# The TensorE program of an expert-choice MoE, written out instead of looped

## The chip, the cores and the metric

The kernel runs on one core of a Trainium2 chip. Its metric is the device time of one execution, in microseconds (us), given as the median of three runs. The profile is of one further execution.

## The reference

One inference step of a backbone with one layer. 512 latent tokens (`x_sample`) and 128 context tokens (`x_prompt`), each 1024 wide, go through a mixing sub-layer (pooling and retention) and then a mixture of 16 experts in which each expert picks its tokens: the top 64 latent and the top 16 context tokens. All weights are float32.

```python
aff = softmax(h @ w_router)                      # one row of 16 scores per token
gate, idx = top_k(swapaxes(aff, 1, 2), cap)      # each expert picks its tokens
xs = h[idx]
hid = silu(xs @ w_gate) * (xs @ w_up)            # 1024 -> 2816, per expert
out = (hid @ w_down) * gate                      # 2816 -> 1024, per expert
y = zeros.at[idx].add(out)
```

The outputs are the normed rows of both token sets and the retention states of the context.

## The kernel before

The mixing sub-layer comes first (up to about 600 us) and is not touched. After it come the experts. An expert's hidden width of 2816 is cut in two, so that there are 32 half experts (`STEPS = 2 * NE`). The weights of a half expert come in 12 pieces of 1.0 to 1.6 MB: four of the gate matrix (`g`), four of the up matrix (`u`), four of the down matrix (`d`). They are read through a ring of 12 buffers (`RING`, the tile `ring`). SyncE issues each load at L568 (gate and up) or L575 (down), once TensorE has counted the buffer's last reading on the semaphore `e_used`; a load that has landed is counted on `e_landed[slot]`.

TensorE runs the pieces in the order of `STEP`: g0, d0, g1, d1, g2, d2, d3, g3, u0, u1, u2, u3. The gate and up pieces are those of half expert r + 1, the down pieces those of half expert r. The gate product is done in two parts: units of tokens against the weights themselves (L2396) and units against sums of weight blocks (L2403). The sums are made by VectorE (L1715, tile `sums`) from the gate pieces in the ring, ahead of TensorE. The down products are at L2386 and the up products at L2414. Every half expert issues 776 pairs of a weight load and a matmul by the counts of the trace.

TensorE's first eight pieces stand ahead of the loop. Then the loop `pe.Fori(0, STEPS - 1)` at L2423, a loop that the engine itself executes, goes 31 times through the 12 pieces, and its waits are on semaphore values that are computed from the loop's register r. The last down pieces are behind the loop (L2458). SyncE, GpSimd, VectorE and ScalarE have loops of their own over 15 experts (L594, L823, L1885, L1217), with two half experts in each pass.

In each pass GpSimd gathers the token rows of the next expert (L756 and L766, indirect DMAs into `x_g`) and adds the rows of the expert before to a scratch in DRAM (L800 and L803). The gather lies in the even half experts, r = 0, 2, 4 and so on up to 28.

Behind the experts GpSimd reads the summed rows into `y_tile` (L837). That waits for the landing of the last down piece, since `y_tile` lies where ring buffers were. ScalarE and VectorE norm the rows, and the outputs are written.

Of the kernel before, what the change touches and what calls it, by code (L numbers as in the profile page):

```python
# [54 lines left out]
STEPS = 2 * NE  # L55
# [191 lines left out]
def build(nc, x_prompt, x_sample, c, state_ret, c_ctx, w_ada, b_ada, norm1_g, w_in, w_pool, pool_scale,  # L247
# [3 lines left out]
    with ctx:  # L251
# [1686 lines left out]
        def _(pe):  # L1938
# [365 lines left out]
            def gate_up(up, i, slot, tiles):  # L2304

                w = ring[slot][:, 0:2 * FH].rearrange("p (k f) -> p k f", f=FH)
                for kk in range(2):
                    k = 2 * i + kk
                    for x in tiles:
                        for c in range(4):  # L2310
                            ins = mm(bank[UP_BANK[x] if up else x][c * Q:(c + 1) * Q, 0:FC], xs_t[:, x, k * Q:(k + 1) * Q],  # L2311
                                     w[:, kk, c * FC:(c + 1) * FC], start=k == 0, stop=k == KT - 1)
                return ins
# [65 lines left out]
            def down(i, slot):  # L2379

                w = ring[slot][:, 0:DOWN_N[i] * D].rearrange("p (f d) -> p f d", d=D)
                for j in range(DOWN_N[i]):
                    f = DOWN_AT[i] + j
                    for x in range(NX):
                        for c in range(4):
                            ins = mm(bank[5 + x // 2][c * Q:(c + 1) * Q, x % 2 * DC:(x % 2 + 1) * DC],  # L2386
                                     hid_t[:, f, x * Q:(x + 1) * Q], w[:, j, c * DC:(c + 1) * DC],
                                     start=f == 0 and x != 1, stop=f == FTH - 1, skip_group_check=True)
                ins.then_inc(e_used, 1)

            def gate(r, i, slot):

                w = ring[slot][:, 0:2 * FH].rearrange("p (k c n f) -> p k c n f", k=2, c=4, n=2)
                for u, b, o, k, n in OWN_AT:
                    for c in range(4):
                        mm(bank[b][c * Q:(c + 1) * Q, o:o + FN], unit(u)[:, i, :], w[:, k, c, n, :],  # L2396
                           start=i == 0 and o == 0, stop=i == KT // 2 - 1, skip_group_check=True)
                for j in range(N_SUM):
                    b, o = SUM_AT[j]
                    if j % 2 == 0:  # L2400
                        pe.wait_ge(sums_done, 4 * N_SUM * r + N_SUM * i + j + 2)
                    for c in range(4):
                        ins = mm(bank[b][c * Q:(c + 1) * Q, o:o + FN], unit(j)[:, i, :], sums[:, (N_SUM * i + j) % SUM_SLOTS, c, :],  # L2403
                                 start=i == 0 and j % 2 == 0, stop=i == KT // 2 - 1, skip_group_check=True)
                ins.then_inc(e_used, 1)

            def up(i, slot):

                w = ring[slot][:, 0:2 * FH].rearrange("p (k f) -> p k f", f=FH)
                for x in range(NX) if i else reversed(range(NX)):  # L2410
                    for kk in range(2):
                        k = 2 * i + kk
                        for c in range(4):
                            ins = mm(bank[UP_BANK[x]][c * Q:(c + 1) * Q, 0:FC], xs_t[:, x, k * Q:(k + 1) * Q],  # L2414
                                     w[:, kk, c * FC:(c + 1) * FC], start=k == 0, stop=k == KT - 1)
                    if i == 3 and x < 2:
                        ins.then_inc(e_up, 1)
                ins.then_inc(e_used, 1)

            pe.wait_ge(e_xt, 1)  # L2420
            for t in range(FIRST):
                gate_up(t // 4, t % 4, t, (0, 1)).then_inc(e_used, 1)
            with pe.Fori(0, STEPS - 1) as r:  # L2423
                for t in range(RING):
                    slot = (FIRST + t) % RING
                    kind, i = STEP[t]
                    if t == 0:
                        pe.wait_ge(x_dve, r + 1)
                        pe.wait_ge(x_act, r + 1)
                        pe.wait_ge(e_silu, 2 * r + 2)  # L2430
                        pe.wait_ge(e_comb, r + 1)
                    if (kind, i) == ("d", 0):
                        pe.wait_ge(e_hid, NX * r + NX)
                    if (kind, i) == ("u", 0):
                        pe.wait_ge(e_xt, r + 2)
                        pe.wait_ge(e_out, NX * r + NX)
                    pe.wait_ge(e_landed[slot], 16 * r + (16 if slot >= FIRST else 32))
                    if kind == "g":
                        gate(r, i, slot)
                    elif kind == "d":  # L2440
                        down(i, slot)
                    else:
                        up(i, slot)
# [86 lines left out]
```

## Time and profile before

| what | value |
|---|---|
| median of 3 runs | 1986.44 us (1984.62 to 1986.86) |
| profiled execution, its own time | 1986.42 us |
| its span, first to last instruction | 1984.6 us |
| TensorE busy in matmuls | 1910.4 us, 96% of the span |
| VectorE, ScalarE, GpSimd busy | 1207.5, 395.4, 394.6 us |
| mean granted TensorE clock | 0.989 of full speed |
| read from HBM, written to it | 632.47 MB, 14.40 MB |

The span leaves out 1.8 us that the execution's own time has around it. A share of busy time is a mean over stages: the experts take about 640 to 1953 us, and there both TensorE and the DMA engines are busy nearly all the time. The page says of every DMA queue how many packets it moved, how many MB, and what share of the 16 DMA engines' time they took. One of the queues carries instructions. Times of rows count from the span's start.

### The profile page before, as it was taken

To read this page: it belongs to the slowest core of one execution; us is meant where nothing else is said; L and a number is where in the kernel's file an instruction comes from. 1 tells how busy PE (TensorE), PEld (TensorE's weight loads), DVE (VectorE), ACT (ScalarE), POOL (GpSimd) and SP (SyncE) were. 2 spreads that over 40 slices of the span, in tenths; PEclk is the share of its full clock that TensorE was granted. 3 is DMA by queue.
4 is the path that set the end of the run, shared out by engine and by line. 5 is a ranking of instruction groups with operands and counts; after the bars stand their busy time and mean duration, and the time that the engine had idled before them with its cause. 6 is when DMAs were issued, how large, how long until landed. Compare 5 with 4: busy or idle time off the path is not lost.

```text
span 1984.6 us, 64364 instructions
## 1 busy us (share of the span) xinstructions
PE 1910.4 (96%) x28594; PEld 1604.4 (81%) x28594; DVE 1207.5 (61%) x1969; ACT 395.4 (20%) x909; POOL 394.6 (20%) x406
## 2 busy tenths in 40 slices
PE   8999999999997999999999999999999999999996
PEld 5888899999873888788877778779777687877874
DVE  3532441232556777687676867767677676867764
ACT  4331333122320111111111211112111111211113
POOL 3032019000411130311303113030211303112012
PEclk9999999999998999999999999999999999999998
DMA  8244542312359999999999999999999999999997
GB/s 334 86 161 151 176 129 64 107 51 79 127 220 363 412 407 419 408 411 415 408 418 409 414 412 411 415 407 420 407 411 416 407 419 408 412 414 412 414 411 288
DMA packets 150463, 647.58 MB, mean 326 GB/s; under 512 B 11420, under 2 KB 56344, under 8 KB 134024
## 3 DMA queue, kind: packets, MB, share of 16 engines
q1 hardware_dynamic: 134576, 617.71, 77.5%
q0 software_dynamic: 15648, 29.02, 5.0%
q8 instruction: 42, 0.69, 0.1%
q14 instruction: 13, 0.11, 0.0%
q10 hardware_dynamic: 184, 0.06, 0.0%
HBM read 632.47 MB, written 14.40 MB: 326 GB/s over the span
## 4 chain that ended last, share of the span: by engine, by line
PE 76%; DMA 12%; DVE 4%; SPq 3%; issue 3%; ACT 1%; POOL 0%; POOLq 0%; DVEq 0%; ACTq 0%
PE bank L2386 17%; PE bank L2414 16%; PE bank L1985 16%; PE bank L2403 9%; DMA ring<-in_w_exp_gate_dram 9%; PE bank L2396 6%; PE bank L2106 3%; PE bank L2252 2%; SPq L568 2%; DMA ring<-in_w_exp_down_dram 1%; PE bank L2311 1%; SPq L575 1%; PE bank L1956 1%; PE bank L1967 1%; DMA x_in<-in_x_sample_dram 1%
## 5 line engine op out<-in xcount | busy, mean ns | idle before, releaser
L1715 DVE TENSOR_TENSOR sums<-ring 128x704 f32<-128x704 f32 x744 | 608.5, 886 | 191.8 <-PE bank L2403 168.2
L2386 PE MATMUL bank<-ring,hid_t 128*32 128x256 f32 x8184 | 480.4, 379 | 12.9 <-DVE hid_t L1787 7.2
L2414 PE MATMUL bank<-ring,xs_t 128*32 128x352 f32 x5952 | 453.1, 459 | 0.0
L2386 PEld LDWEIGHTS bank<-ring,hid_t 128*32 128x32 f32 x8184 | 380.6, 110 | 79.4 <-issue 9.8
L2414 PEld LDWEIGHTS bank<-ring,xs_t 128*32 128x32 f32 x5952 | 307.5, 110 | 128.3 <-issue 7.6
L2403 PE MATMUL bank<-sums,xu_a 128*32 128x176 f32 x5952 | 296.5, 313 | 18.3 <-issue 17.8
L2403 PEld LDWEIGHTS bank<-sums,xu_a 128*32 128x32 f32 x5952 | 241.9, 110 | 42.6 <-issue 40.3
L791 POOL TENSOR_TENSOR small<-kpow 128x2 f32<-128x2 f32 x31 | 10.4, 334 | 993.1 <-DVE out_rows L1846 868.1
L1167 ACT ACTIVATE v_both<-bank 128x176 f32<-128x176 f32 x31 | 9.9, 318 | 856.0 <-PE bank L2403 856.0
L2396 PE MATMUL bank<-ring,xu_a 128*32 128x176 f32 x1984 | 173.8, 313 | 0.0
L1985 PE MATMUL bank<-act_hi,wt_hi 128*128 128x320 f32 x448 | 138.8, 310 | 0.8 <-DVE rtmp L1526 0.8
L1276 DVE TENSOR_TENSOR wt_lo<-raw_t,wt_hi 128x2048 fp32r<-128x2048 f32 x25 | 57.6, 2303 | 134.6 <-ACT wt_hi L888 134.6
L1985 PE MATMUL bank<-act_lo,wt_hi 128*128 128x320 f32 x448 | 138.4, 309 | 0.0
L1985 PE MATMUL bank<-act_hi,wt_lo 128*128 128x320 f32 x448 | 138.4, 309 | 0.0
L2396 PE MATMUL bank<-ring,xu_b 128*32 128x176 f32 x1984 | 123.9, 313 | 0.0
L2396 PEld LDWEIGHTS bank<-ring,xu_a 128*32 128x32 f32 x1984 | 114.1, 110 | 9.8 <-issue 0.3
L2396 PEld LDWEIGHTS bank<-ring,xu_b 128*32 128x32 f32 x1984 | 94.2, 110 | 1.6
L803 POOL DMA_INDIRECT acc_scratch<-out_rows,idx_scatter x60 | 83.2, 1386 | 18.3 <-issue 18.3
L1985 PEld LDWEIGHTS bank<-act_hi,wt_hi 128*128 128x128 f32 x448 | 84.1, 188 | 1.3 <-issue 1.3
L1985 PEld LDWEIGHTS bank<-act_lo,wt_hi 128*128 128x128 f32 x448 | 84.1, 188 | 0.0
L1985 PEld LDWEIGHTS bank<-act_hi,wt_lo 128*128 128x128 f32 x448 | 84.1, 188 | 0.0
L1189 ACT ACTIVATE silu_g<-bank 128x352 f32<-128x352 f32 x31 | 14.4, 465 | 233.2 <-PE bank L2414 233.2
(366 smaller groups left out, 2398.5 us busy)
## 6 DMA issues: line engine op xcount, KB each, us to landing
ring<-in_w_exp_gate_dram SPq DMA_DIRECT2D x128, 1408.0 KB
ring<-in_w_exp_up_dram SPq DMA_DIRECT2D x128, 1408.0 KB
ring<-in_w_exp_down_dram SPq DMA_DIRECT2D x96, 1536.0 KB
ring<-in_w_exp_down_dram SPq DMA_DIRECT2D x32, 1024.0 KB
raw_t<-in_w_ada_dram SPq DMA_DIRECT2D x16, 1024.0 KB, 5.3
raw_t<-in_w_in_dram SPq DMA_DIRECT2D x14, 1024.0 KB, 5.2
a_raw<-in_w_ada_dram SPq DMA_DIRECT2D x8, 1024.0 KB, 16.5
raw_t<-in_w_branch_gate_dram SPq DMA_DIRECT2D x8, 1024.0 KB, 5.4
```

The source lines that it names most:

```text
L568: sp.dma_start(ring[slot][:, 0:2 * FH].rearrange("p (k f) -> p k f", f=FH), src).then_inc(e_landed[slot], 16)
L575: sp.dma_start(ring[slot][:, 0:DOWN_N[i] * D], src).then_inc(e_landed[slot], 16)
L803: pool.indirect_dma_start(acc_rows, bass.IndirectOffsetOnAxis(idx_scatter[0:C_P, 2 + c:3 + c], 0), out_rows[prompt_slots(c), 2, :], None, ...
L1276: nc.vector.tensor_tensor(lo_of(b), raw(INDEX[b]), hi_of(b).bitcast(F32), ALU.subtract).then_inc(w_lo_done, 1)
L1715: nc.vector.tensor_tensor(sums[:, (N_SUM * i + j) % SUM_SLOTS], w[:, k, :, n, :], w[:, kk, :, nn, :], ALU.add if sign > 0 else ALU.subtrac ...
L1985: ins = mm(out, a, b, start=i == 0, stop=i == count - 1)
L2106: return mm(o[:, :], a, w, start=i == first and kk == 0 and z == 0, stop=i == last and kk == 1 and z == 2)
L2252: return mm(bank[WO_BANKS[i % 3][c]][:, :], a, w, start=k == 0 and z == 0, stop=k == KT - 1 and z == 2)
L2386: ins = mm(bank[5 + x // 2][c * Q:(c + 1) * Q, x % 2 * DC:(x % 2 + 1) * DC], hid_t[:, f, x * Q:(x + 1) * Q], w[:, j, c * DC:(c + 1) * DC], ...
L2396: mm(bank[b][c * Q:(c + 1) * Q, o:o + FN], unit(u)[:, i, :], w[:, k, c, n, :], start=i == 0 and o == 0, stop=i == KT // 2 - 1, skip_group_ ...
L2403: ins = mm(bank[b][c * Q:(c + 1) * Q, o:o + FN], unit(j)[:, i, :], sums[:, (N_SUM * i + j) % SUM_SLOTS, c, :], start=i == 0 and j % 2 == 0 ...
L2414: ins = mm(bank[UP_BANK[x]][c * Q:(c + 1) * Q, 0:FC], xs_t[:, x, k * Q:(k + 1) * Q], w[:, kk, c * FC:(c + 1) * FC], start=k == 0, stop=k = ...
```

## The change

The loop on the engine becomes a loop in the Python program that builds the kernel, so that TensorE's instructions for the 31 half experts stand one after another, and the values waited for are constants.

```diff
@@ -2420,7 +2420,7 @@
             pe.wait_ge(e_xt, 1)
             for t in range(FIRST):
                 gate_up(t // 4, t % 4, t, (0, 1)).then_inc(e_used, 1)
-            with pe.Fori(0, STEPS - 1) as r:
+            for r in range(STEPS - 1):
                 for t in range(RING):
                     slot = (FIRST + t) % RING
                     kind, i = STEP[t]
```

The order of the matmuls and the conditions of the waits stay the same. The loops of the other engines stay.

## Rows read from the trace of the kernel before

**Rows 1.** The page's 40 slices of the span: busy tenths, and GB/s.
```profile
PE   8999999999997999999999999999999999999996
...
DMA  8244542312359999999999999999999999999997
GB/s 334 86 161 151 176 129 64 107 51 79 127 220 363 412 407 419 408 411 415 408 418 409 414 412 411 415 407 420 407 411 416 407 419 408 412 414 412 414 411 288
```
**Rows 2.** The windows view: us, busy us by engine (x instructions), PEclk, DMA share, GB/s.
```profile
640.00:684.40 44.40, 42.34 (x788) 35.20 (x780) 30.59 (x52) 5.93 (x20) 7.14 (x7) 1.00 1.02 411
684.40:768.60 84.20, 82.50 (x1558) 71.00 (x1553) 61.59 (x97) 12.43 (x37) 15.78 (x14) 1.00 1.02 412
...
1189.10:1273.40 84.30, 82.47 (x1560) 66.34 (x1556) 61.32 (x97) 12.44 (x37) 15.85 (x14) 1.00 1.02 412
...
1699.40:1785.10 85.70, 82.83 (x1557) 68.02 (x1553) 61.32 (x97) 12.43 (x37) 16.29 (x14) 1.00 1.02 412
...
1870.40:1910.80 40.40, 40.40 (x784) 36.97 (x780) 29.30 (x44) 6.04 (x16) 8.97 (x7) 1.00 1.03 410
```
**Rows 3.** The chain that ended last, in order of time: start us, us, what.
```profile
1283.66 3.67 PE bank L2386 x68
...
1370.63 26.23 DMA ring<-in_w_exp_gate_dram
...
1883.67 26.31 DMA ring<-in_w_exp_gate_dram
...
1927.19 29.27 DMA ring<-in_w_exp_down_dram
1956.75 4.43 DMA y_tile<-acc_scratch
```
**Rows 4.** The groups view of TensorE's lines in the loop: xcount, busy us, mean ns.
```profile
L2386 PE MATMUL bank<-ring,hid_t 128*32 128x256 f32 x8184 | 480.4, 379 | 12.9 <-DVE hid_t L1787 7.2 <-issue 5.0 <-DVE hid_t L1822 0.6
L2414 PE MATMUL bank<-ring,xs_t 128*32 128x352 f32 x5952 | 453.1, 459 | 0.0
...
L2403 PE MATMUL bank<-sums,xu_a 128*32 128x176 f32 x5952 | 296.5, 313 | 18.3 <-issue 17.8
...
L2396 PE MATMUL bank<-ring,xu_a 128*32 128x176 f32 x1984 | 173.8, 313 | 0.0
```
**Rows 5.** The page's queues: packets, MB, share; and its first section.
```profile
PE 1910.4 (96%) x28594; PEld 1604.4 (81%) x28594; DVE 1207.5 (61%) x1969; ACT 395.4 (20%) x909; POOL 394.6 (20%) x406
...
q8 instruction: 42, 0.69, 0.1%
```
**Rows 6.** The DMA view of 700 to 1950 us: the queues.
```profile
q1 hardware_dynamic: 80115, 505.67, 98.4%
q0 software_dynamic: 9437, 9.76, 3.6%
q14 instruction: 2, 0.02, 0.0%
```
**Rows 7.** The DMA view of 640 to 684.4 us, half expert 0.
```profile
q1 hardware_dynamic: 2849, 17.83, 98.5%
q0 software_dynamic: 224, 0.33, 2.1%
q8 instruction: 7, 0.11, 1.0%
```
**Rows 8.** The DMA view, queue q1, from 724.8 and from 893 us, 44.4 us each.
```profile
q1 hardware_dynamic: 2893, 18.08, 99.2%
...
q1 hardware_dynamic: 2854, 18.12, 99.4%
```
**Rows 9.** The DMA view in narrow windows: 628.4 to 629.3, 701.3 to 702.2, 702.2 to 703.5 us.
```profile
DMA packets 64, 0.32 MB, mean 360 GB/s; under 512 B 16, under 2 KB 16, under 8 KB 56
...
DMA packets 65, 0.39 MB, mean 437 GB/s; under 512 B 7, under 2 KB 7, under 8 KB 55
...
DMA packets 75, 0.59 MB, mean 455 GB/s; under 512 B 9, under 2 KB 9, under 8 KB 42
```
**Rows 10.** The timeline of TensorE's matmuls across the end of a pass at 1061.33 us.
```profile
1047.13 14.43 PE L2414 MATMUL bank<-ring,xs_t 128*32 128x352 f32 x192
1061.33 0.52 PE L2396 MATMUL bank<-ring,xu_a 128*32 128x176 f32 x8
```
**Rows 11.** The source view of L2403: what TensorE's idle time before it ended with.
```profile
  issue: 58.1, 136
```

## The prediction

> **What bounds the kernel now.** I read the slices first. From the fourteenth slice on, about 645 us, both TensorE and the DMA engines stand at nine tenths or more to the end [rows 1]. Two engines can't both be the bound over the same stretch unless they are nearly equal, so the question is which of them gives way to the other.
>
> The windows by pairs of half experts answer that. I cut the stretch at TensorE's own steps, where its first gate matmul begins (640.4, 684.4, 768.6 us and so on). The reader should see two lengths. Until about 1357 us a pair takes 84.0 to 84.3 us, and after it 85.3 to 85.7 [rows 2]. The DMA share and the rate are the same in both: 1.02 of the 16 engines' time and 412 GB/s. So the DMA engines work at their limit all the way, from before 700 us, while TensorE's pace changes. A half expert with no gather takes 40.4 us at best, with TensorE busy through all of it [rows 2] (the last row).
>
> The weights thus come more slowly than TensorE uses them in the first eight pairs. It lives on a store of landed pieces, since the ring had been filled ahead. Once the store is down to what VectorE needs for its sums, the DMA engines set the pace. The chain of waits says the same. In the experts it first holds only matmuls, still at 1283 us. From 1370 us it goes, once in each pair, through 26.2 us of a transfer into the ring, seven times, and it ends with the last down piece and the load of `y_tile` behind it [rows 3]. The span's end is therefore the end of the weight stream plus a fixed 28 us: 1927.2 + 29.3 = 1956.5, and 1984.6 less that.
>
> What follows for any edit: time taken from TensorE in this stage buys nothing, and every microsecond given to the DMA engines for something else comes back in full, also in the first part, where TensorE is the slower to notice.
>
> **What is removed.** Gone are 31 jumps back and the register operations that computed the waits' values. Their price on the path: nothing. Across the end of a pass the last up matmul starts just ahead of 1061.33, and the row of up matmuls (1047.13 + 14.43 = 1061.56 us, with the tail of the last) runs into the first gate matmul of the next pass at 1061.33 with no gap [rows 10]. The half expert of 40.4 us busy in 40.4 us has both a jump and all its register waits inside [rows 2]. What covers them is TensorE's queue of matmuls already issued. If that cover were gone, the DMA limit would still stand ahead of it. The bound from the other side is all of TensorE's idle time that ended with nothing but its own issuing, 58.1 us [rows 11]. Its stretches lie in even half experts only, inside the gather, not at the jump, and I give the change none of them: nothing is removed at that place, and the DMA engines would not let the gain through.
>
> **What is added.** The instructions themselves have to be read. First their number. The four lines of the loop have 8184 + 5952 + 5952 matmuls and, at L2396, 1984 for each of two operands [rows 4], so 24056, or 776 pairs in each of 31 passes. The page has 28594 pairs and 42 packets of instructions on queue q8 [rows 5]. If each was read once, written straight it is 28594 - 30 x 776 = 5314 pairs, 10628 instructions, and 10628 / 42 = 253 for a packet of 0.69 / 42 MB = 16.4 KB. That the loop's body is read once and then kept is to be seen directly: 7 packets in the first pass [rows 7], about 1552 / 253 = 6.1 by the count, and not one on q8 in the 1250 us from 700 to 1950 [rows 6]. After the change all 31 passes are like the first: 30 x 1552 / 253 = 184 more packets, 3.0 MB.
>
> The Trainium skill ("Runtime: NRT & Kernel Launch", "Instruction fetch mechanics") has 16 KiB blocks of 256 instructions too, and 128 KiB for TensorE, enough for this body. It also says that crossing a block boundary is mostly hidden, and that a kernel should rather be unrolled, since a jump out of the window stalls. By that rule the change costs nothing or gains, which is among the rivals below.
>
> Then the price of a packet. TensorE doesn't wait for one: it reads ahead, and the first pass shows no gap of its own (42.3 us busy of 44.4, with the gather's idle time in it like every even pass). The price is paid by the weight stream. Two measures bound it.
>
> - Below: the 7 packets took 1.0% of 16 engines' 44.4 us [rows 7], so 0.01 x 16 x 44.4 / 7 = 1.01 us of one engine each. Spread over 16 engines that is 63 ns of the stream.
> - Above: what the stream moved less. In 44.4 us of the first pass q1 moved 17.83 MB [rows 7]. In equal windows placed alike in two later even passes it moved 18.08 and 18.12 [rows 8]. That is 0.25 to 0.29 MB less, at about 408 KB a us 0.61 to 0.71 us, or 88 to 102 ns for each packet.
>
> Is it right to divide by 16? A ring transfer ends with one small packet from each engine. At 628.4 us all 16 of them lie in one 0.9 us window. At 701 us, after the packets of the first pass, 7 engines are on time and 9 come in the 1.3 us behind it [rows 9], some 1.1 us late by the windows' middles. So packets go to one engine after another, each making one more late, and don't pile up on one. A lateness of 1.1 us over 16 engines is 69 ns a packet, between the two measures.
>
> I take 86 ns: close to the measures of the stream itself, since lost ring bytes are what counts, and a little below them because the windows' edges cut pieces. 184 x 0.086 = 15.8 us. The ends are 184 x 0.063 = 11.6 and 184 x 0.102 = 18.8.
>
> The sum: 1986.42 (profiled, 0.02 from the median of the runs) + 15.8 = 2002.2 us. The pair of half experts goes from 85.5 to 85.5 + 12.27 x 0.086 = 86.6 us in the part that the DMA engines set. As the first part's 84.2 falls further behind, the store is used up sooner: it fell 1.3 us a pair over eight pairs, it will fall 2.4, so the chain should turn to ring transfers after four or five pairs, at 1000 to 1100 us instead of 1360.
>
> **The rivals.**
>
> - *The packets are hidden.* If the stream made up for them, say because the engines had slack between pieces, the time would stay at 1986.4. For it speaks only that 3.0 MB is 0.5% of the traffic. Against it: a DMA share of 1.02 with no slack [rows 2] and the late engines [rows 9]. For less than 0.2% (4.0 us) a packet would have to cost under 22 ns. Chance 0.05. That the change doesn't do what it says has no way to happen here that I can see; it would also give this time.
> - *TensorE waits for its instructions.* Reading ahead works in the first pass, but every pass now needs it under a full DMA load. If each of 184 packets stalled it by the 1.01 us that the packet takes, TensorE's pair would be 84.2 + 12.4 = 96.6, and the end 15.5 x (96.6 - 85.5) = 172 us later, about 2158. If it stalls for a tenth of that (1.2 us a pair) it stays under the DMA pace of 86.6 and costs nothing; it decides from 0.2 us a packet on. Chance 0.06, mostly near the lower end.
> - *All packets after the first pass go to one engine.* Then that engine has 184 x 1.01 = 186 us more to do, and as each transfer waits for its slowest share the end is at about 2160. [rows 9] speak against it. Chance 0.01.
> - *Faster, through TensorE.* The jump and the register operations keep TensorE's sequencer from running ahead, and this is why it starves during gathers. Written out it would not, and up to 58.1 us of idle time [rows 11] would go: 1928. The mechanism decides only if the DMA engines could move in 80.8 us (twice 40.4) what they now move in 85.5 us at 412 GB/s, which is 436 GB/s, and no window shows it [rows 2]. Chance 0.02.
> - *Faster, through the jump.* Each jump back waits for a packet of its target, 1.01 us: 30 us less, 1956. The skill's rule on jumps, named above, would have this. No packet on q8 for 1250 us [rows 6] and no gap at 1061.33 [rows 10] rule it out as it stands. Chance 0.01.
>
> **How the numbers follow.** My forecast has 0.85: slower by 11.6 to 18.8 us, 1998.0 to 2005.2. About 4 us (0.2%) is what a measurement of this kernel tells from no change. Slower: 0.85 + 0.06 + 0.01 = 0.92. Same: 0.05. Faster: 0.03. For the range I widen the bounds of the price by 2 us below, for packets that cost less where the stream is refilled between passes, and by 3.8 above for short stalls of TensorE: 1996.0 to 2009.0.
>
> **What the profile after should show.** About 226 packets (3.7 MB) on q8, and some 6 of them in each 42 us from 640 to 1950. A DMA share of 1.02 as before, and a rate of about 409 GB/s where it was 412. Half experts with no gather still at 40.4 us before the DMA engines take over, and pairs of 86.6 us after. The last down piece landing near 1972 us, and 28 us behind it. TensorE's instructions the same in number. I am wrong if gaps of TensorE stand where packets land, if the pairs stay at 85.5, or if one engine's share grows late without end.

## The result and the profile after

The kernel takes 2018.2 us (median of 4 runs, 2016.6 to 2020.4) where the one before takes 1985.9 (4 runs). The ratio is 1.0164 with a 95% interval of 1.0146 to 1.0182, so 32.4 us slower. The direction was as forecast and the amount was twice the forecast one: 15.8 us had been expected.

The page after, its slices from the head (the granted clock, the DMA engines, the rate):

```profile
PEclk8999999999988999999999999999999999999998
DMA  8254532212369999999999999999999999999995
GB/s 337 80 162 141 175 125 79 89 64 84 138 255 362 414 404 409 413 406 415 405 413 411 409 407 398 412 400 405 408 408 403 396 417 397 404 410 408 405 400 233
...
q8 instruction: 224, 3.67, 0.7%
```

The instruction queue has 182 packets more than in [rows 5], 3.0 MB, where 184 were counted beforehand. The rate starts at about 409 GB/s and is often 396 to 405 in the later slices, where [rows 1] have 407 to 420.

The windows by pairs of half experts, cut again at TensorE's own steps:

```profile
641.60:723.40 81.80, 81.15 (x1557) 50.46 (x1553) 62.28 (x99) 11.96 (x36) 16.64 (x14) 1.00 1.02 409
723.40:804.20 80.80, 80.80 (x1556) 59.36 (x1552) 59.05 (x93) 12.42 (x37) 15.87 (x14) 1.00 1.02 409
804.20:886.60 82.40, 81.15 (x1559) 59.47 (x1555) 59.04 (x95) 12.41 (x37) 16.93 (x14) 1.00 1.02 409
886.60:975.20 88.60, 82.60 (x1556) 67.43 (x1552) 61.98 (x98) 12.43 (x37) 15.89 (x14) 0.96 1.02 411
...
1151.60:1240.30 88.70, 83.65 (x1560) 47.48 (x1556) 61.18 (x96) 12.41 (x37) 16.19 (x14) 0.96 1.01 404
...
1851.90:1940.40 88.50, 83.30 (x1558) 49.63 (x1554) 61.11 (x96) 12.42 (x37) 16.45 (x14) 0.96 1.01 405
```

Two things differ from [rows 2]. The first pairs are at 80.8 to 82.4 us where they were 84.2: TensorE's idle time in the gathers is nearly gone. And from 886.6 to 1851.9 us eleven pairs take 87.75 us each where the forecast was 86.6. In most of those the DMA share has fallen by a hundredth, and the mean granted clock of TensorE is 0.96 to 0.98.

The chain of waits, in order of time:

```profile
775.95 27.44 DMA ring<-in_w_exp_gate_dram
...
1915.31 26.29 DMA ring<-in_w_exp_gate_dram
1959.72 29.63 DMA ring<-in_w_exp_down_dram
1989.64 4.19 DMA y_tile<-acc_scratch
```

It turns to ring transfers at 776 us instead of 1370 [rows 3]. The last down piece lands at 1989.3 and the span ends 27.9 us later, as before. The end is the end of the weight stream here too, so all of the 32.4 us has to be found in the stream.

It is found in two places. From 700 to 1950 us the DMA view of after has this:

```profile
q1 hardware_dynamic: 78785, 496.09, 97.2%
q0 software_dynamic: 9376, 9.51, 3.6%
q8 instruction: 175, 2.87, 0.9%
```

Against 505.67 MB in [rows 6], q1 moved 1.9% less in the same time. Over the 1312 us of the stage in the kernel before (640 to 1952 us) that is 24.9 us. The packets took 0.009 x 16 x 1250 / 175 = 1.03 us each, the 1.01 of before.

The second place is the end of the stream. Windows of 4 us up to the last landing, with each engine's busy time and, at the row's end, the granted clock, the mean DMA share and the rate; before:

```profile
1940.00:1944.00 4.00, 4.00 (x60) 1.81 (x56) 3.37 (x7) 3.41 (x8) 0.03 (x1) 1.00 1.00 422
1944.00:1948.00 4.00, 4.00 (x60) 1.70 (x54) 0.00 (x0) 0.04 (x1) 3.67 (x6) 1.00 1.01 425
1948.00:1952.00 4.00, 4.00 (x60) 1.82 (x56) 0.70 (x2) 0.00 (x0) 1.94 (x2) 1.00 1.02 425
1952.00:1956.00 4.00, 3.72 (x68) 2.20 (x60) 2.99 (x5) 1.95 (x3) 0.00 (x0) 1.00 0.92 322
```

and after:

```profile
1973.00:1977.00 4.00, 4.00 (x60) 1.65 (x56) 3.60 (x7) 3.42 (x9) 0.00 (x0) 1.00 0.50 207
1977.00:1981.00 4.00, 4.00 (x60) 1.60 (x56) 0.00 (x0) 0.27 (x1) 3.50 (x6) 1.00 0.76 294
1981.00:1985.00 4.00, 4.00 (x60) 1.64 (x56) 0.52 (x1) 0.00 (x0) 2.12 (x3) 1.00 0.68 246
1985.00:1989.00 4.00, 3.72 (x64) 2.15 (x60) 3.15 (x5) 1.95 (x3) 0.00 (x0) 1.00 0.40 154
```

Before, the 16 engines work in full until 4 us from the end and finish together. After, about half of them are done some 16 us early, and the last transfers wait for the rest. In the last 16 us the share is short by 0.50, 0.25, 0.34 and 0.52 of 4 us each, 6.4 us per engine. 24.9 + 6.4 = 31.3 of the 32.4 us. So the instruction packets do not lie on all engines alike.

The trace shows directly how they lie. For most transfers into the ring it keeps sixteen times of landing, one for each engine's share (for some a few are missing). The table has how far each share lands behind the transfer's first one, in us; the kernels of the last five rows are described below.

| kernel | first share lands at | seven shares | one share | the other eight |
|---|---|---|---|---|
| before | 702.0 | up to 0.3 | 1.0 | 1.5 to 1.9 |
| before | 1872.5 | up to 0.3 | 1.0 | 1.1 to 1.7 |
| after | 703.0 | up to 0.4 | 1.0 | five 1.5 to 2.0, three 3.0 to 3.3 |
| after | 1112.3 | up to 0.7 | 1.7 | 12.7 to 14.4 |
| after | 1972.6 (the last) | up to 0.3 | 0.3 | 13.7 to 16.8 |
| first8 | 1016.0 | up to 0.7 | 1.9 | 10.5 to 11.3 |
| first8 | 1884.2 | up to 0.6 | 1.7 | 10.3 to 11.4 |
| last15 | 1298.3 | up to 0.3 | 1.6 | 1.6 to 1.9 |
| last15 | 1953.3 (the last) | up to 0.5 | 1.7 | 13.9 to 17.2 |
| light_straight | 1387.8 | up to 0.4 | 0.5 | 0.6 to 2.7 |

From 630 to 689 us eight packets come in the kernel before, and with each of them one more share falls behind, until eight are. In the changed kernel the ninth packet (689.1 us) takes one of the late ones to 3.2 us, and the seven stay where they are. So the packets go round on eight of the sixteen engines. The sixteenth share, 1.0 us late, is so before the second packet comes; what makes it late is not shown.

### The profile page after: what moved, and what is told of

Its sections match the earlier page's. It is cut to its first block, busy times and chain, and to the rows that moved or that the text cites. A ratio compares the mean times of both kernels' runs of the same rounds, so it can differ in the third digit from the quotient of the medians.

```text
span 2017.2 us, 63743 instructions
## 1 busy us (share of the span) xinstructions
PE 1913.1 (95%) x28594; PEld 1379.1 (68%) x28594; DVE 1207.6 (60%) x1969; ACT 394.9 (20%) x909; POOL 397.2 (20%) x406
## 3 DMA queue, kind: packets, MB, share of 16 engines
q8 instruction: 224, 3.67, 0.7%
## 4 chain that ended last, share of the span: by engine, by line
PE 64%; DMA 21%; DVE 5%; SPq 5%; issue 2%; ACT 1%; POOL 0%; DVEq 0%; POOLq 0%; ACTq 0%
DMA ring<-in_w_exp_gate_dram 19%; PE bank L2386 16%; PE bank L1985 15%; PE bank L2414 11%; PE bank L2403 6%; PE bank L2396 4%; SPq L568 3%; PE bank L2106 3%; PE bank L2252 2%; SPq L575 2%; DMA ring<-in_w_exp_down_dram 1%; PE bank L2311 1%; DVE hid_t L1780 1%; PE bank L1956 1%; PE bank L1967 1%
## 5 line engine op out<-in xcount | busy, mean ns | idle before, releaser
L2386 PE MATMUL bank<-ring,hid_t 128*32 128x256 f32 x8184 | 487.3, 394 | 62.6 <-DVE hid_t L1787 62.0
L2386 PEld LDWEIGHTS bank<-ring,hid_t 128*32 128x32 f32 x8184 | 276.3, 114 | 246.2 <-DVE hid_t L1787 66.8
L2414 PEld LDWEIGHTS bank<-ring,xs_t 128*32 128x32 f32 x5952 | 225.2, 110 | 207.3 <-issue 160.3
L2403 PE MATMUL bank<-sums,xu_a 128*32 128x176 f32 x5952 | 249.7, 313 | 0.0
L2403 PEld LDWEIGHTS bank<-sums,xu_a 128*32 128x32 f32 x5952 | 193.6, 110 | 32.3
L2396 PE MATMUL bank<-ring,xu_a 128*32 128x176 f32 x1984 | 129.1, 313 | 0.0
L2396 PE MATMUL bank<-ring,xu_b 128*32 128x176 f32 x1984 | 101.5, 313 | 0.0
L2396 PEld LDWEIGHTS bank<-ring,xu_a 128*32 128x32 f32 x1984 | 70.7, 110 | 29.1 <-issue 6.6
L2396 PEld LDWEIGHTS bank<-ring,xu_b 128*32 128x32 f32 x1984 | 66.9, 110 | 11.1
L766 POOL DMA_INDIRECT x_g<-h_scratch,idx_gather x60 | 57.4, 956 | 18.3 <-issue 18.3
## 6 DMA issues: line engine op xcount, KB each, us to landing
a_raw<-in_w_ada_dram SPq DMA_DIRECT2D x8, 1024.0 KB, 16.3
```

Of the source, the lines that this page charges most:

```text
L766: pool.indirect_dma_start(x_g[prompt_slots(c), 2, :], None, source, bass.IndirectOffsetOnAxis(idx[0:C_P, 2 + c:3 + c], 0)).then_inc(e_gath ...
```

## The experiments

Two theories stood against each other. Theory A: about half of the DMA engines get all the packets; a transfer lands with its slowest share, so each packet costs 0.176 us from the first on, and the cost is linear in their number. Theory B: the packets are even and cost 0.086 us, and the other half of the loss comes only after the store of landed pieces is used up, through TensorE's idle time and its lower clock.

In the runs that change the form of the loop, its body is made a function `half_expert(r)`, and what calls it differs. The edits of light_loop and few_waits are made to the kernel before.

**First eight written out.**
```diff
-            with pe.Fori(0, STEPS - 1) as r:
+            for r in range(8):
+                half_expert(r)
+            with pe.Fori(8, STEPS - 1) as r:
+                half_expert(r)
```


> Half experts 0 to 7 written out, 8 to 30 in a loop: 8 x 6.13 = 49 more instruction packets than before. Theory A (the packets fall on a part of the 16 DMA engines, each transfer ends with the slowest of them, so each packet costs the stream 32.4 / 184 = 0.176 us from the first on): 49 x 0.176 = 8.6 us slower, 1994.5. Theory B (the packets are even, 0.086 us each, and the rest of the loss comes only after the store of landed pieces is used up, when TensorE idles in the even half experts, falls to half clock and frees buffers late): 49 x 0.086 = 4.2 us slower, 1990.1, and nothing more since the store is hardly used up by half expert 8.

Measured: 1994.3 us against 1986.2 on the same chip, ratio 1.0045 (1.0031 to 1.0059), 8.1 us slower with 49 packets more. That is 0.165 us a packet. B's 4.2 us is outside the interval (6.2 to 11.7 us). The end of this kernel's stream, some 930 us after the last packet that the loop read in its own first pass (1016 us):

```profile
1948.00:1952.00 4.00, 4.00 (x68) 1.88 (x64) 2.78 (x6) 3.10 (x10) 0.00 (x0) 1.00 0.88 370
1952.00:1956.00 4.00, 4.00 (x60) 1.61 (x56) 1.35 (x3) 1.55 (x3) 2.05 (x4) 1.00 0.59 233
1956.00:1960.00 4.00, 4.00 (x60) 1.63 (x56) 0.00 (x0) 0.00 (x0) 3.09 (x5) 1.00 0.74 288
```

The engines' shares stand apart at the end although 22 of the loop's 23 passes ran without packets. The landings say the same: the late eight are 10.5 to 11.3 us behind at 1016 us and 10.3 to 11.4 at 1884. The reader should see that lateness taken on early is not given back here: each engine has its share of every transfer to move, at full load, and nothing evens them out.

**First sixteen, and last fifteen, written out.** The same edit with 16 for 8, and with the loop over 0 to 16 ahead of the written part.

> Half experts 0 to 15 written out, the rest in a loop: 98 more packets. A: 98 x 0.176 = 17.2 us slower, 2003.1, the shares of a transfer ever further apart up to half expert 15 and staying so after it. B: 8.4 us for the packets and about 1.2 us for each of the five pairs after half expert 6, 14.4 us, 2000.3.

> Half experts 0 to 15 in a loop, 16 to 30 written out: 15 x 6.13 = 92 more packets. A: 92 x 0.176 = 16.2 us slower, 2002.0, with the engines' shares of a transfer together up to half expert 16 and apart by up to 15 us at the end. B: 7.9 us for the packets, and 1.2 us for each of the seven pairs, 16.3 us as well; the two differ in where the shares of a transfer part, not in the time. In both the gather's idle time of TensorE (issue, at L2403) stands in the even half experts of the loop and not in those written out, if register operations cause it.

Measured: 2003.2 us, ratio 1.0090 (1.0074 to 1.0105), 17.0 us for 97 packets, and 2002.0 us, ratio 1.0080 (1.0065 to 1.0095), 15.8 us for 91 packets. Both are within 0.5 us of A. For first16 B's 14.4 us is just below the interval (14.7 to 20.9). For last15 B had 16.3 us, so its time can't tell the two apart; its landings do. The shares lie together as in before up to 1298 us and are 13.9 to 17.2 us apart at the end, as A said, so it is the packets that part them. One expectation missed: the idle time in gathers, meant to stand in the looped part, is 1.0 us in last15. More on it below.

**Two half experts in the body.**
```diff
+            with pe.Fori(0, NE - 1) as n:
+                half_expert(2 * n)
+                half_expert(2 * n + 1)
+            half_expert(STEPS - 2)
```


> A loop on the engine with two half experts in its body, 15 times, and one behind it: a body of 12.3 packets. If TensorE keeps only some 8 packets (or any number below 12), every pass reads all anew: about 220 packets on q8 and 32 us slower (A and B), 2018, with the register operations kept. If it keeps 12 or more, 48 packets and 1986.

Measured: 2028.7 us, ratio 1.0213 (1.0196 to 1.0229), 42.5 us slower, worse than no loop at all. Its page has

```profile
q8 instruction: 250, 4.10, 0.8%
```

so a body of 12.3 packets isn't kept, every pass reads it again, and more than it: 208 packets above before instead of 182. The expected 32 us came too low, because here the jump costs. The chain of waits at the end of one pass:

```profile
1069.98 6.80 PE bank L2414 x92
1076.79 4.68 issue
1081.47 2.57 PE bank L2396 x32
```

TensorE stands still for 4.7 us between the last up matmul and the first gate matmul. The 14 jumps back cost 61.2 us of such gaps in all, 4.4 us each. The Trainium skill ("Runtime: NRT & Kernel Launch", "Instruction fetch mechanics") says that a jump whose target is outside the current window of two pages stalls for the fetch. The trace agrees for this body. A body of 6.1 packets is longer than two pages as well, and [rows 10] show no stall there; the measurement decides. In this kernel the stream is not the bound. Its chain of waits, by engine, has no transfer into the ring:

```profile
PE 65%; issue 4%; DVE 0%; POOL 0%; DMA 0%; POOLq 0%; ACT 0%; DVEq 0%
```

Two windows, over the gap and behind it, have the granted clock in the third column from the end:

```profile
1076.80:1081.40 4.60, 0.00 (x0) 0.00 (x0) 2.15 (x5) 0.46 (x1) 1.30 (x3) 0.90 1.02 421
1081.47:1085.00 3.53, 3.53 (x50) 2.38 (x54) 0.00 (x0) 0.00 (x0) 2.62 (x4) 0.50 1.02 421
```

TensorE sets the pace: a pair took 88.5 to 89.0 us, which is its 80.8, the 4.4 of the gap and, as an estimate, half of the 6.8 us in which the granted clock behind the gap is 0.50. So the 42.5 us are not a price of packets and don't stand in the table of prices below.

**Lighter loads.** Of u1, u2 and u3 in the 31 half experts only half of each piece is loaded; the matmuls stay and run on what lies in the buffer, so the outputs are not those of the reference. Once with the loop, once written out.
```diff
-                sp.dma_start(ring[slot][:, 0:2 * FH].rearrange("p (k f) -> p k f", f=FH), src).then_inc(e_landed[slot], 16)
+                n = 1 if up and i and half + ahead else 2
+                sp.dma_start(ring[slot][:, 0:n * FH].rearrange("p (k f) -> p k f", f=FH), src[:, 0:n]).then_inc(e_landed[slot], 16)
```


> Loop as before, but the loads of u1, u2 and u3 of the 31 half experts bring half of their piece (704 of 1408 KB; the matmuls run on what the buffer holds): 12.5% less for the DMA engines, about 75 us a pair where TensorE needs 84.2. Both theories: TensorE-bound throughout, 15.5 pairs at 84.0 to 84.2 instead of 84.2 and later 85.5, about 10 to 13 us faster than before: 1974.

> The same lighter loads with the program written out. The DMA engines have room for the packets in this one, even for the slowest engine (75 + 2.3 us a pair against TensorE's 80.8). If the jump and register operations cause TensorE's idle time in gathers, it goes, and written out is faster than the loop with the same loads by about 3.4 us for each of 15 pairs, 50 us: 1924. If packets stalled TensorE it would be slower than light_loop.

Measured: 1921.8 us (1921.1 to 1922.6) with the loop and 1924.2 (1921.7 to 1927.3) written out. Their ratios to before, 0.9671 (0.9655 to 0.9688) and 0.9690 (0.9674 to 0.9706), overlap. The 182 packets that cost 32.4 us in the full kernel cost 2.4 by the medians when the stream has room, and that is not clear of the noise. So the packets don't hold up TensorE: from 640 to 1875 us of 1235 it is busy in 1234.4 with the loop and in 1234.3 written out, and it sets the pace in both. The chain by engine, written out:

```profile
PE 67%; issue 1%; DVE 0%; POOL 0%; DMA 0%; POOLq 0%; ACT 0%; DVEq 0%
```

The same 182 packets leave the sixteen shares of any transfer within 4.5 us here, where the full kernel has them up to 18.2 us apart: with room, the late engines catch up. A pair of half experts in the middle of each, first the loop, then written out:

```profile
1367.90:1448.60 80.70, 80.70 (x1556) 50.40 (x1552) 61.20 (x97) 12.43 (x37) 15.94 (x14) 1.00 0.98 383
```

and

```profile
1366.90:1447.60 80.70, 80.70 (x1556) 50.48 (x1552) 61.17 (x97) 12.41 (x37) 15.94 (x14) 1.00 0.99 388
```

TensorE is busy in 80.7 of 80.7 us in both, so the jump and the register waits of light_loop cost nothing. My expectation of 84.2 us a pair and 1974 us for the loop was wrong, since the gather's idle time did not come.

**Register waits, without a jump back.** Written out, each half expert inside a loop of one trip.
```diff
-            for r in range(STEPS - 1):
+            for n in range(STEPS - 1):
+                with pe.Fori(n, n + 1) as r:
```


> Written out, but each half expert stands in a loop of one trip, so that its waits are computed from a register as in the loop of before, and nothing jumps back. Instruction packets as in the changed kernel (some 3 more). If the register operations cause TensorE's idle time in gathers, that is back (even half experts of about 43.8 us at the start); if the jump back caused it, it stays away. The time is set by the DMA engines in either case: about 2018 by theory A; by theory B the same.

Measured: 2018.8 us, ratio 1.0166 (1.0148 to 1.0184), 224 packets. The same as the changed kernel. The idle time in gathers is not back (1.2 us), so register operations alone don't cause it.

**Fewer register waits, in the loop.**
```diff
-                    if j % 2 == 0:
-                        pe.wait_ge(sums_done, 4 * N_SUM * r + N_SUM * i + j + 2)
+                    if j == 0:
+                        pe.wait_ge(sums_done, 4 * N_SUM * r + N_SUM * i + N_SUM)
```


> The loop of before with one wait on VectorE's sums for each gate piece instead of three, so that 8 register operations of 14 go from each half expert and no instruction packet comes. If they cause the idle time in gathers, it shrinks, even half experts at the start are nearer to 40.4 than to 43.8 us, and the store is used up sooner. The time stays at 1986, since the DMA engines set it; within 3 us either way.

Measured: 1985.5 us, ratio 0.9998 (0.9988 to 1.0007). The idle time at L2403 is gone entirely, the half experts from 684 to 846 us take 40.4 us each, with a gather or without, and the time did not move. This is the plainest sign that time taken from TensorE isn't worth anything here. It doesn't show that the register operations caused the idle time, as the next runs make clear.

**The kernel before, again, and all but the last half expert in the loop.**

> The kernel before, profiled once more. Its first profile has 58.1 us of TensorE's idle time under issue at L2403, in the gathers; the kernels with the same register operations in their waits (one_trip, the loop part of last15, few_waits) have about 1 us. If the program causes it, it is here again, about 58 us. If it belonged to that one execution, there is about 1 us here and the span is the same within 3 us, since the DMA engines set it: even half experts of 40.4 us at first, then a store used up sooner (by 850 to 900 us instead of 1360) and pairs of 85.5 us.

> Half experts 0 to 29 in a loop, the last one written out: 6.1 instruction packets more than before, read once in the last 85 us. Price by theory A: 6.1 x 0.176 = 1.1 us, 1987.0, within what can be told from before. It also asks whether TensorE's idle time in the gathers (58.1 and 73.1 us under issue at L2403 in two profiles of before, about 1 us in last15 with the same loop body over 16 trips) belongs to the loop as such: about 60 us here if it does, about 1 us if it needs something else that before has and this one lacks.

A second profile of the kernel before, an execution of 1987.5 us, has 73.1 us under issue at L2403 (58.1 in [rows 11]), so it wasn't an accident of one execution. With that much idle time TensorE sets the pace itself: the chain of that profile is 66% PE and has no transfer into the ring. In the kernel before the two limits thus lie within a few microseconds of each other. The loop over 30 with the last half expert written out, 1988.4 us and ratio 1.0013 (1.0003 to 1.0022), has 69.1 us of it. The idle time is there in before and in but_last, and is 0 to 1.2 us in every other run. light_loop has the very program of before on TensorE, and last15 has its loop body and its loads. Neither the register operations, nor the jump, nor the load alone explains it. Its cause stays open.

The price of a packet over the kernels with full loads that the stream bounds:

| kernel | packets more | slower, us | us a packet |
|---|---|---|---|
| but_last | 6 | 2.6 | (0.6 to 4.4 us in all) |
| first8 | 49 | 8.1 | 0.165 |
| last15 | 91 | 15.8 | 0.173 |
| first16 | 97 | 17.0 | 0.175 |
| the changed kernel | 182 | 32.4 | 0.178 |
| one_trip | 182 | 32.6 | 0.179 |

## Why the prediction was wrong

**What held.** The stream bounds the kernel: few_waits freed TensorE of all its idle time in the gathers for nothing, and the light kernels removed the cost of the packets. The number of packets (184 forecast, 182 found), 28 us from the last landing to the end, no gain from the jump, and no stall of TensorE on a packet all held.

**The step that failed** is the one under "Is it right to divide by 16?": "So packets go to one engine after another, each making one more late, and don't pile up on one." The rows behind it [rows 9] showed seven engines on time and nine late. I took that for the middle of a turn over 16 engines. It was the whole turn: the packets go round on eight engines, and the others never get one. The landings show it: after eight packets eight more shares are late, the ninth makes one of the late ones later, and the seven are within 0.3 us of the first in the last transfer. With the mean price of 0.086 us over 16 engines the packets cost the eight that take them 0.086 x 16 / 8 = 0.17 us of the stream each, and a transfer ends with those eight. So the term that was mis-sized is the price of a packet: 0.086 us was put in, and the five kernels of the table with 49 or more packets measured 0.165 to 0.179.

The trace doesn't name the engine of a packet; that there are eight rests on the sixteen landings, on the price, and on the halved share at the end of the stream. What stays open is why a packet costs its engine more than its own 1.03 us: in first8 the late eight fell back by some 9.5 us for 49 / 8 = 6.1 packets each, 1.5 us a packet, and the time grew by 8.1 / 6.1 = 1.3.

**How the term divides.** Of the 32.4 us, 6.4 are the early end of the idle half. The 1.9% that the stream moved less in the middle, 24.9 us, has three parts by the queues' shares before [rows 6] and after. The packets themselves held 0.9%, 11.8 us. All queues together fell from 102.0% to 101.7%, about 4 us in which engines idled: a likely reason, not shown, is that the engines without packets run ahead until no further load is issued for them. The remaining 9 us are in the ring's own transfers: q1's share fell by 1.2% where its bytes fell by 1.9%, so a byte took 0.7% longer. Its cause is open. The shares are rounded to a tenth of a percent, which is 1.3 us.

**The rivals.** Packets all on one engine (0.01, 2160 us) had the right mechanism at the wrong width. It deserved a middle case, a part of the engines, with the range drawn up to it: 184 x 1.4 / 8 = 32 us, with 1.4 = 0.086 x 16. (Its own sum was a little off: 1986 and 186 make 2172, not 2160.) The sign of being wrong that the prediction named, a share that grows late without end, was there on eight engines at once, up to 18.2 us. TensorE waiting for its instructions did not happen in the changed kernel. Both faster rivals stayed out, though the idle time that one of them would have removed did go from the first pairs (80.8 us for a pair), and was worth nothing, as its counter-argument said. Since TensorE was faster by that idle time and the stream slower than forecast, the chain turned to ring transfers at 776 us and not at 1000 to 1100.

## What to carry to other kernels

A loop on an engine is worth keeping where the DMA engines are full and the body is kept after its first pass: from then on its instructions cost no transfers. Extra traffic is to be priced at the busiest DMA engine, not at the mean of 16, as every transfer lands with its slowest share. Look at the DMA share in the last microseconds of a stream, and at the spread of one transfer's landings, to see whether the engines end together. And a loop whose body is too long to be kept (12.3 packets here, where 6.1 were kept) was the worst of the three forms.

## What the runs showed of the hardware

TensorE's instruction packets went round on eight of the 16 DMA engines: eight shares of each ring transfer fall behind, by up to 18.2 us in after, and the other eight stay within 2.6 us of the first.

Lateness between DMA engines persists at full load: first8 has its late eight 10.5 to 11.3 us behind at 1016 us and 10.3 to 11.4 at 1884 us, with no packet between. With lighter loads it doesn't build up (light_straight, at most 4.5 us).

A mean granted clock of 0.96 stands in the pairs of after in which TensorE waits 5 to 6 us for `hid_t` at the first down piece. There the clock is at the lower level, 1.2 GHz, for some microseconds: from 984.2 to 987.0 us the granted clock is 0.50, from 990.0 on 1.00. The first 72 down matmuls take 5.80 us in the chain of waits there, where [rows 3] have 3.67 for 68. It lies on the chain, but how much of the time it is worth was not measured apart.
